# Product-key retrieval kernel on one Trainium2 core: key-1 one-hot rows from bit codes and a table on TensorE in place of a VectorE comparison

## What is computed

```python
t1, i1 = lax.top_k(s1, PEER_TOPK)          # key 1 of 128
t2, i2 = lax.top_k(s2, PEER_TOPK)          # key 2 of 128
...
expert = jnp.take_along_axis(cand_i, top_pos, axis=-1)   # key1 * 128 + key2, 128 slots for each token
gate = jax.nn.softmax(top_s, axis=-1)
h = jnp.einsum('td,ted->te', xb, u[eb])
a = jax.nn.gelu(h, approximate=False) * gb
y = jnp.einsum('te,ted->td', a, v[eb])
```

## Time and profile before

| | us |
|---|---|
| median of 3 runs | 3013.98 (3012.6 to 3024.54) |
| span of the profiled execution | 3008.3 |
| the search ends, `build_gates` starts | 970.8 |
| first product of step 0 | 984.0 |
| the tile of block 0 goes out | 1017.7 |
| the tile of block 7 goes out | 1306.0 |
| `experts` starts | 1325.3 |

### The profile page before, as it was taken

How to read it: one execution, slowest core, us unless ns; L and a number is a source line. 1 busy time by engine, 2 the same in 40 slices (tenths; PEclk the granted TensorE clock), 3 DMA queues, 4 the chain that set the end, 5 groups by cost and what they waited for, 6 DMA issues and landing times.

```text
span 3008.3 us, 40533 instructions
## 1 busy us (share of the span) xinstructions
PE 2606.9 (87%) x14808; PEld 2026.4 (67%) x14808; DVE 2295.6 (76%) x4830; ACT 1040.8 (35%) x1778; POOL 1610.1 (54%) x1187
## 2 busy tenths in 40 slices
PE   9998888989995666636769999999999999999997
PEld 7796677768774556524436677777777676777775
DVE  5614666658998989946767778778778877779999
ACT  5413433334543777721112223222222222222222
POOL 0010010125885656656666666666676766756774
PEclk9999999999997777868889999999999999999998
DMA  4424212312111999999999999999999999999995
GB/s 150 134 73 149 87 60 74 115 53 78 53 39 62 312 331 321 322 318 408 392 383 385 384 389 384 401 392 398 388 394 373 401 398 404 391 379 350 371 377 207
DMA packets 309825, 833.44 MB, mean 277 GB/s; under 512 B 26144, under 2 KB 114656, under 8 KB 309632
## 3 DMA queue, kind: packets, MB, share of 16 engines
q0 software_dynamic: 150864, 548.60, 47.4%
q1 hardware_dynamic: 158768, 282.31, 26.2%
HBM read 771.93 MB, written 58.88 MB: 276 GB/s over the span
## 4 chain that ended last, share of the span: by engine, by line
PE 18%; DVE 13%; DMA 11%; POOL 7%; issue 6%; ACT 0%; DVEq 0%; ACTq 0%; POOLq 0%
DMA e_u_row<-in_u,ids 11%; POOL hold L2157 5%; DVE e_u_row L2395 3%; PE psum L2233 3%; PE psum L2200 3%; PE psum L2234 3%; PE psum L2235 3%; PE psum L2201 3%; PE psum L2202 3%; PE psum L2248 2%; POOL e_u_row L2148 2%; DVE e_y L2385 2%; DVE e_u_row L2404 2%; DVE e_vl L2353 1%; DVE hold L2404 1%
## 5 line engine op out<-in xcount | busy, mean ns | idle before, releaser
L2148 POOL DMA_INDIRECT e_u_row<-in_u,ids x384 | 486.1, 1266 | 336.5 <-DVE ids L2395 232.2
L2395 DVE CUSTOM_DVE_ANT_0 e_u_row<-e_u_row,hold 128x1024 f32<-128x1024 f32 x384 | 467.9, 1223 | 252.0 <-DMA e_u_row<-in_u,ids 202.9
L2233 PE MATMUL psum<-e_vh,e_ah 128*128 128x512 f32 x1024 | 421.1, 411 | 97.6 <-DVE e_y L2385 78.2
L2157 POOL DMA_INDIRECT hold<-in_v,ids x376 | 430.2, 1144 | 134.0 <-issue 109.1
L2234 PE MATMUL psum<-e_vl,e_ah 128*128 128x512 f32 x1024 | 409.8, 400 | 0.0
L2235 PE MATMUL psum<-e_vh,e_al 128*128 128x512 f32 x1024 | 408.1, 398 | 0.0
L2200 PE MATMUL psum<-x1d,e_uh 128*128 128x512 f32 x864 | 341.0, 395 | 0.0
L2201 PE MATMUL psum<-x1d,e_uh 128*128 128x512 f32 x864 | 337.2, 390 | 0.0
L2233 PEld LDWEIGHTS psum<-e_vh,e_ah 128*128 128x128 f32 x1024 | 198.2, 194 | 205.6 <-DVE e_y L2385 103.1
L2202 PE MATMUL psum<-x1d,e_ul 128*128 128x512 f32 x864 | 336.3, 389 | 0.0
L2385 DVE TENSOR_TENSOR e_y<-e_y,psum 128x512 f32<-128x512 f32 x464 | 298.9, 678 | 12.5 <-PE psum L2235 10.3
(11 more groups left out here) (410 smaller groups left out, 5571.1 us busy)
## 6 DMA issues: line engine op xcount, KB each, us to landing
e_vr<-in_v SPq DMA_DIRECT2D x128, 512.0 KB
e_ur<-in_uT SPq DMA_DIRECT2D x108, 512.0 KB
s_G<-g_tile SPq DMA_DIRECT2D x8, 4096.0 KB
e_g<-s_G SPq DMA_DIRECT2D x64, 512.0 KB
ids<-in_w_ch SPq DMA_DIRECT2D x17, 512.0 KB, 4.1
s_ch<-p_out POOLq DMA_DIRECT2D x16, 512.0 KB, 3.3
hold<-in_wq SPq DMA_DIRECT2D x16, 512.0 KB, 4.4
hold<-in_v,ids POOLq DMA_INDIRECT x476
```

What stands on the lines that cost most here:

```text
L2148: pool.indirect_dma_start(out=u_ring[n % U_RING][:], out_offset=None, in_=io["u"], in_offset=bass.IndirectOffsetOnAxis(ap=id_u[:, s, k:k + ...
L2157: pool.indirect_dma_start(out=v_ring[m % V_RING], out_offset=None, in_=io["v"], in_offset=bass.IndirectOffsetOnAxis(ap=id_v[:, t:t + 1], a ...
L2233: nc.tensor.matmul(acc, ah[s][j][:, r], vh[s][j][:, c], start=(first and j == 0), stop=False)
L2395: nc.vector.tensor_tensor_reduce(row, row, xs[:, s, :], 1.0, 0.0, ALU.mult, ALU.add, hs[:, s, k:k + 1]).then_inc(dotted, 1)
```

## The change

The first two steps (`DIRECT = 2`) still compare on VectorE. For the other 30, each first key is written as 7 bits and a constant row, 8 rows in bf16. Multiplied with a table of 8 x 128 whose columns hold twice the bit less one, and minus the number of set bits, this gives 0 where the column is the key and -1 or less elsewhere; ScalarE adds 1 and takes the relu, and that is the one-hot. The bits are made on VectorE, put in order by ScalarE, stored to a scratch tensor in DRAM and read back with the code rows on 8 partitions, 32 KB for a step in runs of 256 bytes. TensorE makes the products of the step after next behind each of the four groups of a step, four matmuls to one of two PSUM banks, and ScalarE evacuates them behind each tile bank. ScalarE makes 5 weighted rows and VectorE 11. All the new transfers are on SyncE's queue.

```diff
@@ -62,11 +62,14 @@
 C_ALL = C_LEVEL + (LEVELS - 1) * 64
+C_CODE = C_ALL
+BITS = 7
+PLANES = BITS + 1
...
-    c = np.zeros((P, C_ALL), np.float32)
+    c = np.zeros((P, C_CODE + NK), np.float32)
     i, j = np.arange(P)[:, None], np.arange(P)[None, :]
@@ -82,6 +85,9 @@
     c[:, C_EPS + 2] = L2_EPS
+    bits = (np.arange(NK)[None, :] >> np.arange(BITS)[:, None]) & 1
+    c[0:BITS, C_CODE:] = 2 * bits - 1
+    c[BITS, C_CODE:] = -bits.sum(axis=0)
     c[:, C_EPS + 3] = L2_EPS * P
@@ -218,7 +224,7 @@
                 load_w(b // 2 + 1, b % 2, b + 2)
-            sp.dma_start(mats[:], io["consts"][:, C_TRIU:]).then_inc(mixer_in, 16)
+            sp.dma_start(mats[:], io["consts"][:, C_TRIU:C_ALL]).then_inc(mixer_in, 16)
             for dst, src in zip(sides, ("sinks", "dt_bias", "a_log")):
@@ -1764,7 +1770,8 @@
         R = 16
-        R_ACT = 7
+        R_ACT = 5
+        DIRECT = 2
         STEPS = TD // R
@@ -1776,6 +1783,17 @@
         iota_in = sem("g_iota_in")
+        codes = [hold[0:PLANES, 10 + s, :].bitcast(BF16).rearrange("p (n k) -> p n k", n=R) for s in range(2)]
+        spare = gt[1].rearrange("p k t -> p (k t)")
+        bit = spare[:, 0:BITS * TD].bitcast(U32).rearrange("p (j t k) -> p j t k", j=BITS, t=ND)
+        number = spare[:, BITS * TD:PLANES * TD].bitcast(U32).rearrange("p (t k) -> p t k", t=ND)
+        plane = spare[:, PLANES * TD:PLANES * TD + PLANES * TD // 2].bitcast(BF16).rearrange("p (t j k) -> p t j k", t=ND, j=PLANES)
+        table_raw = sb("g_table_raw", [PLANES, NK])
+        table = sb("g_table", [PLANES, NK], BF16)
+        table_in, table_set = sem("g_table_in"), sem("g_table_set")
+        cast, bits_set, planes_set, codes_out = (sem(f"g_{n}") for n in "key_cast bits_set planes_set codes_out".split())
+        code_in = [sem(f"g_code_in{s}") for s in range(2)]
+        code_mm, code_hot = sem("g_code_mm"), sem("g_code_hot")
         ur = sb("g_ur", [P, KC, P])
@@ -1801,6 +1819,22 @@
             def _(pe):
+                def distances(q, g):
+                    m = 4 * (q - DIRECT) + g
+                    if m == 0:
+                        pe.wait_ge(tr_ev, ND)
+                        pe.wait_ge(v_numbers, 1)
+                        pe.wait_ge(table_set, 1)
+                    if g == 0:
+                        pe.wait_ge(code_in[q % 2], 16 * (q // 2))
+                    if m >= 2:
+                        pe.wait_ge(code_hot, m - 1)
+                    for n in range(4):
+                        last = nc.tensor.matmul(psum[:, 4 + m % 2, n * NK:(n + 1) * NK], codes[q % 2][:, 4 * g + n, :],
+                                                table[:], start=True, stop=True)
+                    last.then_inc(code_mm, 1)
                 for t in range(ND):
@@ -1818,14 +1852,19 @@
                     pe.wait_ge(hot_act[s], q // 2 + 1)
-                    pe.wait_ge(hot1[s], q // 2 + 1)
+                    if q < DIRECT:
+                        pe.wait_ge(hot1[s], q // 2 + 1)
                     for n in range(R):
...
                             pe.wait_ge(evac[n // 4], q)
+                            if q >= DIRECT:
+                                pe.wait_ge(code_hot, 4 * (q - DIRECT) + n // 4 + 1)
                         last = nc.tensor.matmul(psum[:, n // 4, :].rearrange("p (k t) -> p t k", t=4)[:, n % 4, :],
...
                             last.then_inc(mm[s], 1)
+                            if q + 2 < STEPS:
+                                distances(q + 2, n // 4)
                     b, part = divmod(q, PER)
@@ -1848,6 +1887,15 @@
+                def key_bits(t0, t1):
+                    t = slice(t0, t1)
+                    nc.vector.tensor_copy(number[:, t, :], key1[:, NS + t0:NS + t1, :]).then_inc(cast, 1)
+                    dve.wait_ge(cast, 1 + (t0 > 0))
+                    for j in range(BITS):
+                        last = nc.vector.tensor_scalar(bit[:, j, t, :], number[:, t, :], j, 1, ALU.logical_shift_right,
+                                                       ALU.bitwise_and)
+                    last.then_inc(bits_set, 1)
                 def dot_rows(k0, k1):
@@ -1865,6 +1913,8 @@
                 nc.vector.tensor_copy(id_v[:], psum[:, 4, :]).then_inc(v_numbers, 1)
+                nc.vector.memset(plane[:, :, BITS, :], 1.0)
+                key_bits(0, 1)
                 dve.wait_ge(iota_in, 16)
@@ -1876,11 +1926,13 @@
                     last.then_inc(hot2[s], 1)
-                    dot_rows(U_STEP * q, U_STEP * q + U_STEP // 2)
-                    nc.vector.tensor_tensor(one1[s][:], iota.unsqueeze(1).broadcast_to([P, R, NK]),
-                                            pickT[:, 0, q * R:(q + 1) * R].unsqueeze(2).broadcast_to([P, R, NK]),
-                                            ALU.is_equal).then_inc(hot1[s], 1)
-                    dot_rows(U_STEP * q + U_STEP // 2, U_STEP * (q + 1))
+                    if q < DIRECT:
+                        nc.vector.tensor_tensor(one1[s][:], iota.unsqueeze(1).broadcast_to([P, R, NK]),
+                                                pickT[:, 0, q * R:(q + 1) * R].unsqueeze(2).broadcast_to([P, R, NK]),
+                                                ALU.is_equal).then_inc(hot1[s], 1)
+                    dot_rows(U_STEP * q, U_STEP * (q + 1))
+                    if q == 0:
+                        key_bits(1, ND)
                     if q % PER == 0:
@@ -1899,12 +1951,13 @@
                 pool.wait_ge(v_numbers, 1)
+                pool.wait_ge(code_mm, 4 * (STEPS - DIRECT))
                 for m in range(2 + U_RING, V_RING):
...
                     gather_v(2 + n)
-                pool.wait_ge(hot1[1], STEPS // 2)
+                pool.wait_ge(hot1[1], DIRECT // 2)
                 pool.wait_ge(hot2[1], STEPS // 2)
@@ -1936,17 +1989,36 @@
+                def planes(t0, t1):
+                    act.wait_ge(bits_set, 1 + (t0 > 0))
+                    nc.scalar.activation(plane[:, t0:t1, 0:BITS, :], bit[:, :, t0:t1, :].rearrange("p j t k -> p t j k"),
+                                         ACT.Copy).then_inc(planes_set, 1)
+                def hot_codes(q, g):
+                    m = 4 * (q - DIRECT) + g
+                    act.wait_ge(code_mm, m + 1)
+                    nc.scalar.activation(one1[q % 2][:, 4 * g:4 * g + 4, :],
+                                         psum[:, 4 + m % 2, :].rearrange("p (n k) -> p n k", n=4), ACT.Relu,
+                                         bias=cst[:, C_ONE:C_ONE + 1]).then_inc(code_hot, 1)
                 pick_rows(0)
+                planes(0, 1)
+                act.wait_ge(table_in, 16)
+                nc.scalar.activation(table[:], table_raw[:], ACT.Copy).then_inc(table_set, 1)
+                pick_rows(1)
                 act.wait_ge(iota_in, 16)
                 hot(0)
-                pick_rows(1)
-                hot(1)
                 for t in range(2, ND):
                     pick_rows(t)
+                hot(1)
+                planes(1, ND)
                 for b in range(TD // TG):
...
                     nc.scalar.activation(uh[:], ur[:], ACT.Copy).then_inc(u_hi, 1)
+                    if b == 1:
+                        act.wait_ge(codes_out, 32)
                     act.wait_ge(stored[b % 2], 16 * (b // 2))
@@ -1955,6 +2027,8 @@
                                                  ACT.Copy).then_inc(evac[n], 1)
+                            if q + 2 < STEPS:
+                                hot_codes(q + 2, n)
                         if q + 2 < STEPS:
@@ -1972,16 +2046,45 @@
                 sp.dma_start(xs[:, 0, :], scr["x1"][0:P, :]).then_inc(x_in[0], 16)
-                for b in range(TD // TG):
+                sp.dma_start(table_raw[:], io["consts"][0:PLANES, C_CODE:C_CODE + NK]).then_inc(table_in, 16)
+                def load_u(b):
                     sp.wait_ge(u_lo, b)
                     sp.dma_start(ur[:], io["uT"][AHEAD_R + b]).then_inc(u_in, 16)
+                def store_codes(t0, t1):
+                    sp.wait_ge(planes_set, 1 + (t0 > 0))
+                    sp.dma_start(scr["codes"][t0 * P:t1 * P].rearrange("(t p) j k -> p t (j k)", p=P),
+                                 plane[:, t0:t1].rearrange("p t j k -> p t (j k)")).then_inc(codes_out, 16)
+                def load_codes(q):
+                    if DIRECT <= q < STEPS:
+                        if q >= DIRECT + 2:
+                            sp.wait_ge(code_mm, 4 * (q - DIRECT - 1))
+                        sp.dma_start(codes[q % 2], scr["codes"][q * R:(q + 1) * R].rearrange("t j k -> j t k")
+                                     ).then_inc(code_in[q % 2], 16)
+                load_u(0)
+                sp.wait_ge(numbered, 1)
+                sp.wait_ge(tr, ND)
+                store_codes(0, 1)
+                sp.wait_ge(codes_out, 16)
+                for q in range(DIRECT, DIRECT + 2):
+                    load_codes(q)
+                store_codes(1, ND)
+                sp.wait_ge(codes_out, 32)
+                for b in range(TD // TG):
```

(13 more changed lines are left out.)

## The result

The changed kernel takes 3045.36 us (median of 4 runs, 3040.95 to 3046.73) against 3013.29 us for the kernel before beside it: a ratio of 1.0103, 95% interval 1.0087 to 1.0119. It is 32 us slower where I had forecast 7. That is 0.4 us past the upper end of my range (2975 to 3045), and it falls under "slower by over 0.5%", to which I had given 0.30. The profiled spans are 3044.6 and 3008.3 us.

A forecast was written before the change was run, and what follows sets the result against it. VectorE was taken to bound `build_gates` before the change, at 41.0 us a block. Terms +6 (start), +4 (`x1`), +10 (blocks 1 to 6), -13 (block 7) gave +7 us: 3015 as span, 3021 us as median; range 2975 to 3045.

The forecast's parts named there:

- The queue: Blocks 1 to 6: codes land 28.8 us after the tile's issue; TensorE waits 9 us in each; +10 in all.
- The way from landing to tile: Blocks 1 to 6: from code landing to the next tile's issue, 13.8 us including 0.1 for a wait.
- rival 3: TensorE stays at half clock for both steps after its wait in blocks 1 to 6: +32, 3053 us; chance 0.15.
- The `x1` loads: Block 1: three loads, 1.5 MB, between hidden block and codes cost +4 us at 371 GB/s.
- Block 7: Last block, no codes behind a store: 29.6 us against 42.5, so -13 us.
- The start: Block 0: making and reordering bits sends tile 0 out 6 us later.
- Two of the signs: In `build_gates`: VectorE waiting for rows much above 16 us would show wrong; blocks of 42 to 43 us right.
- Rival 1: Blocks 1 to 6: codes don't wait for the store, blocks take 34.8 us, time 2970 us; chance 0.20.
- Rival 2: Blocks 1 to 6: codes on 8 partitions land earlier, at 25.2 us; time 2999 to 3000 us; chance 0.10.
- Rival 4: Fetched rows bind VectorE during the tile store, block stays at 41 us, time 3011 us; chance 0.10.

The follow-up runs named there:

- e5: Changed kernel with four code buffers in place of two and the first two steps' code loads issued ahead of the tile store: 3005.8 us.
- e1: Changed kernel, still two buffers, with code loads from step 4 on issued by ScalarE on its own queue: 3004.8 us.
- e10: Changed kernel with each tile's store cut to an eighth, the last stage rereading that eighth: 2972.6 us.
- e3: Changed kernel with the three `x1` loads moved from block 1 to block 7, behind the store of tile 6: 3033.0 us.
- e9: Changed kernel with four code buffers, loads ahead of the store, and each tile's store cut to an eighth: 2966.8 us.
- e11: Four-buffer version of the changed kernel, with the next `u` block's load issued by ScalarE on its own queue: 3004.8 us.
- e4: Kernel before, with only five weighted rows on ScalarE and eleven on VectorE: 3019.2 us, ratio 1.0020.

## Why the prediction was right in its mechanism and short in its size

**The queue.** Forecast: codes behind tile and hidden block, landing 28.8 us after the tile's issue (25.2 to 30.1), a wait of 9 us in each of blocks 1 to 6. Measured: the products with those codes start 21.8, 32.9, 25.8, 28.9 and 26.1 us after the tile in blocks 2 to 6, mean 27.1, and 38.5 in block 1 with the `x1` loads. The waits were 17.6 in block 1 and 2.1, 5.8, 4.8, 9.5 and 5.2 us, 7.5 us on average. TensorE came there 19 to 21 us after the tile, as the 20 of the prediction, but once, in block 3, at 27; the waits of 2 and 5 us in blocks 2, 4 and 6 are short because the codes were there earlier than forecast. Mechanism right; e5 and e1 show it.

**The way from landing to tile** is the term that was mis-sized: 13.8 us in the sum, 18.7, 14.5, 16.9, 14.7, 18.1 and 18.2 measured, mean 16.9. Six times 3.1 is 19 us. The sum let three groups of products at half clock pass in 3 x 1.64 us, from the step of 6.57 us in the earlier trace rows. At half clock a group and the small products behind it, which this part of the sum left out, take 2.54 us, from 1235.28 to 1237.82 below: 2.7 us more for the three. The granted clock over that step (1298.8 to 1305.4 us of the kernel before) was 0.56, so it was not at half clock throughout. TensorE's timeline in block 5, after tile 4, a slow one (the small products wait, then groups of 8 records at half clock):

```profile
1234.75 0.60 PE L1834 MATMUL psum<-g_table,hold 8*128 8x128 bf16 x4 [9.49 <-DMA hold<-s_codes]
1235.28 2.08 PE L1862 MATMUL psum<-g_one,g_two 128*128 128x128 f32 x8
...
1237.82 2.08 PE L1862 MATMUL psum<-g_one,g_two 128*128 128x128 f32 x8
...
1240.36 2.08 PE L1862 MATMUL psum<-g_one,g_two 128*128 128x128 f32 x8
...
1246.86 1.05 PE L1862 MATMUL psum<-g_one,g_two 128*128 128x128 f32 x8
...
1248.16 1.16 PE L1862 MATMUL psum<-g_one,g_two 128*128 128x128 f32 x8
...
1250.99 1.16 PE L1862 MATMUL psum<-g_one,g_two 128*128 128x128 f32 x8
```

A group takes 2.08 us through the whole rest of the third step, and only the fourth step runs at 1.16. ScalarE is not what holds it up there; it waits for each of these groups before it can evacuate it:

```profile
1239.93 0.60 ACT L2027 ACTIVATE g_tile<-psum 128x512 f32<-128x512 f32 x1 [1.32 <-PE psum L1862]
```

In block 2, after tile 1, TensorE had waited 2.1 us. The first group still ran at full clock, the second and third slower, and the clock was back before the fourth step; the last two rows are the restarts in the next two blocks:

```profile
1101.14 0.39 PE L1834 MATMUL psum<-g_table,hold 8*128 8x128 bf16 x4 [2.13 <-DMA hold<-s_codes]
1101.46 1.16 PE L1862 MATMUL psum<-g_one,g_two 128*128 128x128 f32 x8
...
1102.88 1.60 PE L1862 MATMUL psum<-g_one,g_two 128*128 128x128 f32 x8
...
1104.95 2.05 PE L1862 MATMUL psum<-g_one,g_two 128*128 128x128 f32 x8
...
1109.62 1.16 PE L1862 MATMUL psum<-g_one,g_two 128*128 128x128 f32 x8
...
1148.55 0.60 PE L1834 MATMUL psum<-g_table,hold 8*128 8x128 bf16 x4 [5.79 <-DMA hold<-s_codes]
...
1191.21 0.60 PE L1834 MATMUL psum<-g_table,hold 8*128 8x128 bf16 x4 [4.84 <-DMA hold<-s_codes]
```

So rival 3 came true for one of the two steps: in four of six blocks all three groups that follow the wait take 2.08 us, and there the way is 16.9 to 18.7 us; in the other two it is 14.5 and 14.7, near my 13.8. I had counted those groups at half clock, though too short, but not the nine hidden products behind them (4.0 us in block 5, 2.2 in the sum), after which ScalarE waits again. I had put the whole rival at +32 us with chance 0.15. The granted clock of the stretch 1020 to 1290 us is 0.77 in the changed kernel and 0.87 in e10, which hardly waits (the clock is the third number from the right):

```profile
1020.00:1290.00 270.00, 207.85 (x1258) 171.81 (x1259) 190.32 (x466) 197.82 (x439) 116.46 (x96) 0.77 0.92 306
```

```profile
1020.00:1290.00 270.00, 218.19 (x1490) 180.75 (x1488) 219.96 (x537) 223.93 (x504) 149.13 (x121) 0.87 0.85 285
```

That the half clock makes most of those 3 us was read from these rows; no run held the clock fixed, so its share is not proven apart.

**The `x1` loads**: 4 us by their bytes, about 9 by e3. In block 1 the products with the codes start 9 us after the landing of the tile store (29.4 us after its issue, against 38.5). The three loads landed 10.0 to 12.6 us after their issue there; 1.5 MB at 371 GB/s had given 4.

**Block 7**: -13 forecast, -5.5 and +3.1 after it. It was priced without transfers, and that failed: e9 and e10, which have few, take 30.7 and 30.8 us there (29.6 forecast), the changed kernel 37.0. I had seen a DMA share of 1.07 and used it in the sum only for the codes.

**The start**: +6 forecast, +4.5. A shift of 384 elements took 0.31 us, not 0.5.

**The 24 us that the sum was short** up to the next stage (31 against 7) are then: the start -1.5; the codes of blocks 2 to 6 there 1.7 us sooner, -8.5; block 1, where they came at 38.5 and not at 28.8 + 4, +5.7; the way to the tile +18.3; block 7 +7.5 and the stretch after it +3.1. Errors of both signs stand in it: with the codes as late as forecast the time would have been some 8 us more, clearly outside the range. That it came so near was luck. Two of the signs that I had named for being wrong or right also came out against me: VectorE waited for rows for 48.2 us, much above 16, and the blocks took 36.3 to 57.2 us and not 42 to 43.

**Rival 1** (codes don't wait, 2970) was wrong twice: they do wait, and without the wait the kernel takes 3003 to 3006, since full engines then bind. **Rival 2** was not seen: the products start 0.6 to 1.4 us behind the landing of the whole hidden block in the three blocks where the trace has it (20.4, 25.2 and 25.3 us after the tile against 21.8, 25.8 and 26.1). So in those blocks the code load's eight partitions did not make it earlier than its predecessor. By the rule of the Trainium skill (DMA: Bandwidth & Descriptors, in the section on why a DMA increments its semaphore by 16) it would be spread over eight engines; whether it was can't be read from these traces. **Rival 4** had the right limit, rows in a full stretch, but as the second bound behind the wait. Most of the gain of the change was eaten. With an eighth of the store the four-buffer kernel is 47 us faster than the kernel before with its full store, but the kernel before was not run with an eighth; with half the store on both sides the difference is 11 us, and with the full store the best versions that compute everything, e1, e5 and e11, keep 7 to 9 us.

## What to carry over

When a step moves work to a path through DRAM, look at what stands ahead of the new loads in their queue before costing their bytes: here 32 KB could be used only 27 us after the issue of the 4 MB store ahead of them, and that place cost 40 us in all; a second queue or two more buffers took that back. Price a stage without a wait only together with what the DMA engines then have to carry: a share near 1 makes the next bound. And price what TensorE does after a forced pause at half clock too, all of it up to the rise: here after waits of 4.8 to 17.6 us it started at half clock, and after one of 2.1 us it fell there in the second group.

## What the runs showed that I had not expected

- Giving VectorE two more weighted rows a step in the kernel before, 18 us of its time, cost only 7 us (e4): an engine that looks like the bound by the waits of others still had waits of its own, 21.0 us here, and they took up 6.5 us of the new work.
- The relu with bias over 128 x 512 takes 0.69 us where the copy takes 0.59 (L2001, L2027), yet back to back the two start 0.52 us apart on average, as I had priced them.
- Blocks of the changed kernel alternate, 36.3, 49.8, 40.4, 46.9, 44.2 us from block 2 on. With the `x1` loads gone from block 1 they are 43.2, 43.7, 43.1, 42.8 and 42.5 (e3), with nearly the same sum. That one late block shook the next five is my reading of one profile of each; why it does is not shown.
